# Past keys with decays relative to the block's first query, three score banks, two projection banks

## The reference

```python
z = x @ w_in                                   # q, k, v, forget logits, gates, conv and memory columns
logf = log_sigmoid(f + fox_bf)                 # 12 heads
cum = cumsum(logf)                             # per head
s = q @ k.T * 128 ** -0.5 + cum[query] - cum[key]
p = softmax(where(key <= query, s, -inf))      # 12 heads x 128
o_fox = p @ v
c = causal_conv3(c_gate * h_in)                # 1536 channels, width 3
o_mem = softmax(mq @ mk.T / 16) @ mv           # 4 heads x 256, 256 memory tokens
m = sum_i sigmoid(x @ w_merge_i + b_i) * ((o_i * silu(g_i)) @ w_out_i)
y = layernorm(2 ** 0.25 * x + m @ w_o) * ln_g + ln_b
```

## Time and profile before

| what | value |
|---|---|
| time, median of 3 (lowest to highest) | 3447.69 us (3447.4 to 3559.09) |
| the profiled execution's own time | 3459.89 us |
| its span, slowest of 8 cores | 3458.3 us (cores 3434.4 to 3458.3) |
| mean granted TensorE clock, cores | 0.984 to 0.990 |
| PE busy | 3329.8 us, 96% |
| DVE, ACT, POOL busy | 35%, 26%, 25% |

### The profile page before, as it was taken

How to read it: one execution, slowest core, us unless ns; L and a number is a source line. 1 busy time by engine, 2 the same in 40 slices (tenths; PEclk the granted TensorE clock), 3 DMA queues, 4 the chain that set the end, 5 groups by cost and what they waited for, 6 DMA issues and landing times.

```text
span 3458.3 us, 54793 instructions; the slowest of 8 cores (3434.4 to 3458.3 us)
## 1 busy us (share of the span) xinstructions
PE 3329.8 (96%) x18998; PEld 1643.9 (48%) x18998; DVE 1198.0 (35%) x1989; ACT 915.5 (26%) x1571; POOL 860.8 (25%) x1045
## 2 busy tenths in 40 slices
PE   7899999999998999999999999999999999999997
PEld 4555555555544444444444444455544444444443
DVE  0476666667676222222211111111112232111465
ACT  1355555455554111111111111111113331111111
POOL 2233333333334222222200000222221113322233
PEclk9999999999999999999999999999999999999999
DMA  9634333433331313131224443866662115665643
GB/s 166 122 74 81 73 81 70 81 70 71 73 66 33 49 25 49 25 49 25 46 58 104 109 92 81 167 152 141 154 144 48 25 25 126 137 144 140 206 151 118
DMA packets 151702, 315.80 MB, mean 91 GB/s; under 512 B 32112, under 2 KB 57328, under 8 KB 146940
## 3 DMA queue, kind: packets, MB, share of 16 engines
q0 software_dynamic: 39232, 134.54, 24.5%
q1 hardware_dynamic: 112200, 177.76, 17.0%
HBM read 351.46 MB, written 95.32 MB: 129 GB/s over the span
## 4 chain that ended last, share of the span: by engine, by line
PE 88%; DMA 4%; issue 2%; DVE 2%; ACT 2%; POOL 1%; POOLq 0%; ACTq 0%; DVEq 0%; SPq 0%
PE bank L146 88%; DMA m_scr<-mt 1%; DMA xT<-xTp 1%; DMA fv_p<-v 1%; ACT ge L163 1%; DVE st L181 1%; DVE acc L173 1%; POOL aC L173 0%; ACT pt L163 0%; POOL pt L169 0%; DMA wcb<-wcM 0%; ACT k L168 0%; ACT rl L163 0%; POOL mt L173 0%; POOL pt L705 0%
## 5 line engine op out<-in xcount | busy, mean ns | idle before, releaser
L146 PE MATMUL bank<-xT,wcb 128*128 128x512 bf16 (+1 forms) x3840 | 728.2, 343 | 7.1 <-DMA wcb<-wcM 6.5
L146 PE MATMUL bank<-xT,cwb 128*128 128x512 bf16 (+1 forms) x3840 | 702.5, 343 | 8.9 <-DVE us L173 8.1
L146 PE MATMUL bank<-xT,wkqg 128*128 128x512 bf16 (+1 forms) x2880 | 608.3, 348 | 8.7 <-DMA wkqg<-wkqg 5.0
L146 PEld LDWEIGHTS bank<-xT,wcb 128*128 128x128 bf16 x3840 | 327.1, 98 | 370.3 <-issue 13.5
L146 PEld LDWEIGHTS bank<-xT,cwb 128*128 128x128 bf16 x3840 | 325.1, 98 | 373.4 <-issue 16.4
L173 DVE TENSOR_TENSOR mt<-bank,gt 128x512 f32<-128x512 f32 (+1 forms) x240 | 143.5, 598 | 1032.5 <-PE bank L146 883.5
L163 ACT ACTIVATE pt<-st,ncc 128x512 bf16<-128x512 f32 (+4 forms) x492 | 314.8, 647 | 427.0 <-DVE st L181 352.0
L163 ACT ACTIVATE gt<-bank,bm 128x512 f32<-128x512 f32 (+1 forms) x240 | 147.0, 612 | 969.0 <-PE bank L146 965.0
L146 PEld LDWEIGHTS bank<-xT,wkqg 128*128 128x128 bf16 x2880 | 245.4, 99 | 274.1 <-issue 35.2
L181 DVE SCALAR_TENSOR_TENSOR st<-bank,cq 128x512 f32<-128x512 f32 x480 | 291.3, 608 | 201.0 <-PE bank L146 172.9
L173 DVE TENSOR_TENSOR acc<-acc,pt 128x512 f32<-128x512 f32 (+3 forms) x396 | 260.7, 658 | 0.9 <-POOL pt L705 0.4
(11 more groups left out here) (137 smaller groups left out, 2543.8 us busy)
## 6 DMA issues: line engine op xcount, KB each, us to landing
m_scr<-mt SPq DMA_DIRECT2D x128, 256.0 KB, 2.2
pv<-m_scr SPq DMA_DIRECT2D x128, 256.0 KB, 5.5
cwb<-wc POOLq DMA_DIRECT2D x12, 2048.0 KB, 16.8
wkqg<-wkqg POOLq DMA_DIRECT2D x11, 1536.0 KB, 15.1
mw<-wm POOLq DMA_DIRECT2D x16, 1024.0 KB, 13.9
x<-xp SPq DMA_DIRECT2D x16, 1024.0 KB, 7.2
y_p<-rr SPq DMA_DIRECT2D x16, 1024.0 KB, 4.8
wcb<-wcC POOLq DMA_DIRECT2D x16, 896.0 KB, 10.8
```

The source lines that it names most:

```text
L146: return lambda e: e.matmul(out, lhsT=lhsT, rhs=rhs, start=start, stop=stop)
```

## The change

- **Scores of past keys.** For a tile that lies wholly before its block, the decay is taken relative to the block's first query: a bias column `nb = ncc + cq[first]`, made on POOL a block (a head) ahead by `make_bias`, so ACT takes the exponential straight from the score bank, with no step on DVE. Diagonal tiles keep the old path. The two parts of a block have output banks of their own; before the first diagonal tile `acc` is scaled by `fq = exp(cq - cq[first])` (`make_decay`, ACT), and at the end the past part's output too, and the parts are added (DVE). The sample's cache tile gets eight exponentials of 64 columns, and its two parts are joined in the same way; `csd` goes.
- **Banks and order.** Score banks 2, 3, 7 (three), projection banks 0, 1 (two) in the attention stage; the sample's output takes a projection bank for its time (`held`). `LA` is 4. A head's blocks come as 0, (sample), 1, 3, 2, in head 0 with the sample after 1; `POS` gives the buffers, `past_block` follows. `st` has 2 buffers, `pt` 9.
- **Block ends.** `hi` is copied on DVE; `lo` is due one tile earlier; Ln and Exp of `rl` are recorded a tile apart. A gate's third and fourth step are due one and two tiles after the first two.
- **Caches.** `load_cache` of the next head follows the sample's value tile (now early in a head), for head 0 the start of the stage.
- **Convolution.** The sample's four groups go one after each 512-token block, with buffers of their own.
- **Layer norm.** The last chunk (the sample) is centred, scaled and stored in four quarters over DVE, ACT and POOL.
- **Prologue.** `q_group(0, 3)` comes before the transposes of the forget logits; rows of `wv0` in SBUF are 288 wide, 268 of them used. `masknegb` was not used and goes.

```diff
-    wvf = [bw("wv0", [128, 16 * 268], BF16, r_vw[0]), ...
+    wvf = [bw("wv0", [128, 16 * 288], BF16, r_vw[0]), ...
...
+    held = set()
+    pjb = [0, 1, 7]
     def nextbank():
-        b = (0, 1, 7)[pj[0] % 3]
-        pj[0] += 1
-        return b
+        while True:
+            b = pjb[pj[0] % len(pjb)]
+            pj[0] += 1
+            if b not in held:
+                return b
...
+        if now[0] is None:
+            log1p()
+            gate()
+        else:
+            later.append((now[0] + 1, log1p))
+            later.append((now[0] + 2, gate))
...
-    run_all(k_group(0, 3))
+    run_all(k_group(0, 3) + q_group(0, 3))
...
-    NST, NPT = 3, 7
+    NST, NPT = 2, 9
...
+        dg = lambda tb: [(h, tb, kc) for kc in range(4 * tb, 4 * tb + 4)]
+        of = lambda tb: [(h, tb, kc) for kc in range(4 * tb)]
+        one, late = of(1) + dg(1), [(h, 4, 0), (h, 4, 1)]
+        tiles += dg(0) + (one + late if h == 0 else late + one) + of(3) + dg(3) + of(2) + dg(2)
...
+    pjb[:] = [0, 1]
+    NB0 = (0, 0, 4, 12, 24)
...
+    def make_bias(h, tb):
+        p = h % 2
+        if tb == 0:
+            return
+        c0, n, k0 = NB0[tb], (4 * tb if tb < 4 else 8), (0 if tb < 4 else 16)
+        ref, rr = (cq[:, tb * 512:tb * 512 + 1], r_cq[tb]) if tb < 4 else (cqs[p][:, 0:1], r_cqs[p])
+        S.add(POOL, TS(nb[p][:, c0:c0 + n], ncc[:, k0:k0 + n, h:h + 1].rearrange("p a b -> p (a b)"), ref, ALU.add),
+              reads=[rr, r_ncc], writes=[r_nb[p][tb]])
+        c = 4 * p + tb - 1
+        S.add(POOL, TS(nr[:, c:c + 1], ref, -1.0, ALU.mult), reads=[rr], writes=[r_nr[p][tb]])
...
-        sb_ = 2 + take("s", 2)
+        sb_ = (2, 3, 7)[take("s", 3)]
...
+            else:
+                c = NB0[tb] + kc
+                S.add(ACT, ACTF(pt[p][:], banks[sb_][:], AF.Exp, bias=nb[h % 2][:, c:c + 1], scale=SCALE),
+                      reads=[bankr[sb_], r_nb[h % 2][tb]], writes=[r_pt[p]])
...
+            for c in range(8):
+                S.add(ACT, ACTF(pt[p][:, c * NS:(c + 1) * NS], banks[sb_][:, c * NS:(c + 1) * NS], AF.Exp,
+                                bias=nb[h % 2][:, 24 + c:25 + c], scale=SCALE),
...
+    def next_decays(i, h, tb):
+        if h + 1 < H:
+            load_cq(h + 1, tb)
+            later.append((i + 8, lambda: make_bias(h + 1, tb)))
...
+            if kc == 4 * tb - 2:
+                make_decay(h, tb)
+            if kc == 4 * tb - 1:
+                S.add(DVE, TT(A[:], A[:], fq[:], ALU.mult), reads=[rA, r_fq], writes=[rA])
             if last:
-                S.add(POOL, COPY(pt[hi][:], A[:]), reads=[rA], writes=[r_pt[hi]])
+                S.add(DVE, COPY(pt[hi][:], A[:]), reads=[rA], writes=[r_pt[hi]])
...
+                    S.add(DVE, TT(fq[:], banks[Of][:], fq[:], ALU.mult), reads=[bankr[Of], r_fq], writes=[r_fq])
+                    S.add(DVE, TT(fq[:], banks[Ob][:], fq[:], ALU.add), reads=[bankr[Ob], r_fq], writes=[r_fq])
+                    finish_block(h, tb, rl[:], r_rl, fq[:], [r_fq], 512)
-                later.append((i + 2, s1))
+                later.append((i + 1, s1))
                 later.append((i + 3, s2))
+                later.append((i + 4, s2b))
+                later.append((i + 6, s3))
...
         elif kc == 0:
+            Ob = nextbank()
+            held.add(Ob)
...
+            make_decay(h, 4)
             if h + 1 < H:
                 load_cache(h + 1)
...
-    LA = 3
+    LA = 4
...
-        for tb, (t0, tn) in enumerate(TBLK):
+        late = []
+        for tb in (4, 0, 1, 2, 3):
...
+            gs = [group(cmm(1, tb), tn, ev_c), group(cmm(2, tb), tn, ev_h), group(cmm(0, tb), tn, ev_b), group(cmm(3, tb), tn, ev_g)]
+            if tb == 4:
+                late = gs
+            else:
+                out += gs[0] + gs[1] + gs[2] + gs[3] + late[tb]
...
-        past_block = [f0 + 5, f0 + 3 + 6, f0 + 11 + 6, f0 + 25 + 6]
+        past_block = [f0 + 5, f0 + 3 + 6, f0 + 29 + 6, f0 + 13 + 6]
...
-            for tb in (4, 3):
-                fill += q_group(n, tb, past_block[3]) + g_group(n, tb, past_block[3])
+            fill += q_group(n, 4) + g_group(n, 4)
+            for tb in (3, 2):
+                fill += q_group(n, tb, past_block[tb]) + g_group(n, tb, past_block[tb])
...
+            center(0)
+            S.add(DVE, lambda e: e.reciprocal(out=rstd[s][0:tn, :], in_=rstd[s][0:tn, :]),
+                  reads=[r_rstd[s]], writes=[r_rstd[s]])
+            scale(POOL, 0)
+            center(1)
+            scale(POOL, 1)
+            center(2)
+            scale(DVE, 2)
+            center(3)
+            scale(DVE, 3)
+            break
```

More of the change, by code:

```diff
@@ L397, in build @@
     qown, gown = [None] * 5, [None] * 5
+    POS = (0, 1, 3, 2)
     r_qs = [Res("qs0"), Res("qs1")]
@@ L484, in build @@
     k32i, v32i, gei = [0], [0], [0]
+    now = [None]
+    later = []
     d_fl = S.dmasem("fl")
@@ L828, in colsof @@
     def colsof(i):
-        h, tb, kc, first, last = tiles[i]
+        h, tb, kc = tiles[i]
         if tb == 4:
@@ L839, in main_pieces @@
         if h == 0:
+            load_cache(0)
+            for tb in range(1, 5):
+                make_bias(0, tb)
             for i in range(LA):
@@ L940, in ev_g @@
                     S.add(DVE, COPY(sx[:, 0:tn], banks[bk][:, 0:tn]), reads=[bankr[bk]], writes=[r_sx, bankr[bk]])
-                    S.add(ACT, ACTF(sc[:, 0:tn], sc[:, 0:tn], AF.Ln, bias=1.0), reads=[r_sc[k]], writes=[r_sc[k]])
-                    S.add(ACT, ACTF(sc[:, 0:tn], sc[:, 0:tn], AF.Exp, scale=-1.0), reads=[r_sc[k]], writes=[r_sc[k]])
-                    S.add(POOL, TT(sc[:, 0:tn], sc[:, 0:tn], sx[:, 0:tn], ALU.mult), reads=[r_sc[k], r_sx], writes=[r_sc[k]])
-                S.add(POOL, TT(aC[c][:, t0:t0 + tn], conv["tb"][k][:, 0:tn], sc[:, 0:tn], ALU.mult),
-                      reads=[r_tb[k], r_sc[k]], writes=[r_aC[c][tb]])
@@ L946, in conv_pieces @@
-            out += group(cmm(1, tb), tn, ev_c)
-            out += group(cmm(2, tb), tn, ev_h)
-            out += group(cmm(0, tb), tn, ev_b)
-            out += group(cmm(3, tb), tn, ev_g)
+                    S.add(ACT, ACTF(sc[:, 0:tn], sc[:, 0:tn], AF.Ln, bias=1.0), reads=[rsc], writes=[rsc])
+                    S.add(ACT, ACTF(sc[:, 0:tn], sc[:, 0:tn], AF.Exp, scale=-1.0), reads=[rsc], writes=[rsc])
+                    S.add(POOL, TT(sc[:, 0:tn], sc[:, 0:tn], sx[:, 0:tn], ALU.mult), reads=[rsc, r_sx], writes=[rsc])
@@ L1400, in build, with root @@
               reads=[r_stat[s]], writes=[r_stat[s]])
-        S.add(ACT, ACTF(rstd[s][0:tn, :], mv[s][0:tn, 1:2], AF.Sqrt, bias=epsb[0:tn, 0:1]),
-              reads=[r_stat[s], r_one], writes=[r_stat[s]])
-        S.add(DVE, lambda e, s=s, tn=tn: e.reciprocal(out=rstd[s][0:tn, :], in_=rstd[s][0:tn, :]),
-              reads=[r_stat[s]], writes=[r_stat[s]])
+        def root(s=s, tn=tn):
+            S.add(ACT, ACTF(rstd[s][0:tn, :], mv[s][0:tn, 1:2], AF.Sqrt, bias=epsb[0:tn, 0:1]),
+                  reads=[r_stat[s], r_one], writes=[r_rstd[s]])
+            S.add(DVE, lambda e: e.reciprocal(out=rstd[s][0:tn, :], in_=rstd[s][0:tn, :]),
+                  reads=[r_rstd[s]], writes=[r_rstd[s]])
```

281 lines of the change are left out of this document (167 added, 114 removed).

## The result

The changed kernel is slower: median 3499.56 us of five runs against 3450.42 us of five runs of the kernel before beside it, ratio 1.0122, 95% interval 1.0107 to 1.0136. That is above the forecast's range (3362 to 3436), a loss where a gain was forecast, and less than the 2% at which the forecast called a change slower.

What follows compares the result with a forecast made beforehand. PE, busy 3329.8 of 3458.3 us, was taken as the bound, leaving only its idle and slow-clock time to win. The terms sum to -44.5 us, taking 3459.9 to 3415.4, or 3403 at the median; range 3362 to 3436.

Steps and rivals of the forecast that it cites:

- the DMA term: Head borders in attention: next head's caches loaded there lengthen the load burst by a fifth; +4 us (0 to +12).
- Borders: Attention stage, between heads: more score banks, longer lookahead and reordered steps cut PE's waits; -24 us (-12 to -40).
- The five releasers: PE's attention waits on score add, `rl`, POOL's `pt` copies and masks, DVE's low `pt`; 48.3 us without the stage's end.
- The rival in which the wait moves to ACT: Borders stay as long because of ACT's exponentials; attention gains nothing; 3428 us at the median, chance 0.22.
- End of the stage: End of attention: the last row sum no longer waits behind the sample's convolution steps; -4 us (-4.9 to 0).
- Clock: Attention stage: shorter borders leave PE less often at the lower clock; -12 us (-20 to 0) of 29 lost.
- The rival of a denser PE held at 0.81: A quarter of the attention stage drops to clock 0.81, cancelling the gain; 3448 us at the median, chance 0.03.
- Two projection banks: Attention projections: small groups wait for evictions, three hand-overs a head; +11 us (0 to 63).
- The rival on two banks: Hand-overs cost 1.9 us each, 63 us, plus clock loss; 3499 us profiled, 3487 at the median, chance 0.05.
- Convolution: Convolution stage: sample matmuls' evictions are covered, chunks 57.2 us apart instead of 58.2; -10 us (-6 to -11.8).
- Tail: Kernel end: last chunk's layer norm and store in quarters over several engines; -7.5 us (-8.5 to -5.5).
- Prologue: Kernel start: `q_group(0, 3)` fills PE's wait for forget logits, against slower `wv0` loads; -2 us (-3.5 to 0).

Runs made afterwards that it cites:

- weights earlier: Changed kernel with the wkqg and wv loads put ahead of the head's first tile, caches left in place; ratio 0.9997 to the kernel before.
- weights later: Changed kernel with the wkqg and wv loads behind the head's 28th tile instead of the 2nd; ratio 0.9890 to the kernel before.
- one exponential: Changed kernel with the sample tile's bias added on DVE and one ACT exponential instead of eight; ratio 1.0063 to the kernel before.

## Why the prediction was wrong, point by point

- **The step that failed is the DMA term.** It counted bytes ("the burst at the border grows by a fifth") and gave +4 (0 to +12). Measured is +64.7 us of PE's wait for `v` (66.2 - 1.5). The step priced the cache load, which costs nothing in the old order, and left out what the tiles moved to the border do to two queues. On POOL's they put a mask that waits for eight exponentials on ACT ahead of the weight loads, which then go out 3.4 us ahead of the V groups and not 9.7; the runs that move the loads alone (weights earlier, weights later) show that this place costs 43 to 80 us. On SP's they put two small transfers ahead of the `v` stores, among the loads; the trace shows these, but no run parts them from the first. POOL's queue was named for the bias columns, not for the loads. The stall itself was known, with its releaser; the step took it for a fixed quantity, where it depends on what is in flight within a few us.
- **Borders,** -24. The five releasers fell from 48.3 us without the end of the stage to 7.8 (4.4 + 3.2 + 0.2 of `pt` on DVE); ACT's `pt` took 24.0 of it back: -16.5, inside the range. The rival in which the wait moves to ACT describes this part, and one exponential takes 22 us off that wait. The eight exponentials were priced too low: 3.17 us, not 2.5.
- **End of the stage,** -4: not won, the last row sum stands 4.30 us behind `sx` now.
- **Clock,** -12: none of it. The mean went the other way, from 0.97 to 0.95; after the stall shown it was at the lower level of 1.2 GHz (0.50 at 516 to 520 us). With the weights later it is 0.99, with one exponential besides 1.00. PE's busy time in the stage says what that is worth: 897.5 us before, 899.2 changed, 870.0 in the last. So nearly all of the 29 us could be had; the forecast left out the stretches at 0.81, and in that last run no window of 4 us shows them. The rival of a denser PE held at 0.81 has no support: at its densest the stage was granted 1.00. (Its sum is a little off too: 3459.9 - 44.5 + 47 is 3450 at the median, not 3448.)
- **Two projection banks,** +11. In the kernel before it costs 22 us, twice the term and within its ends; the hand-overs were under-counted, as the gate's eviction was thought covered and `gr` costs 7.4. In the changed kernel they show as 5.8 for `k` and 1.1 for `gr`, but a third bank, taken from the scores, hid 20 of the 66 us of stalls. The term's reading of a bank as a hand-over missed that it is also a reserve against stalls. The rival on two banks had the side right and the mechanism only in part. That its 3499 in the profile meets the measured 3499.8 is luck: it had 63 us of hand-overs, which measured about 7, and no stalls on stores.
- **Convolution,** -10: -11, and 57.4 us a chunk where 57.2 was forecast. Right.
- **Tail,** -7.5: -3.1. Between `rstd` and the last of DVE's steps 6.3 us passed (3486.19 to 3492.47), not 4.3, as two of them took 1.50 and 1.74 instead of 0.69 beside POOL, and the last store still needed some 5.7 to the end.
- **Prologue,** -2: the wait for the forget logits is gone, but PE's wait for `xT` at the start is 24.5 us instead of 20.5; in other runs of the kernel before and its variants it was 21.7 to 24.5, so no gain or loss can be read. The loads of `wv0` did land later with the gaps: after 15.1 to 17.2 us (the median of a run) in the eleven kernels that have them, after 12.8 to 14.5 in the four without.

Of the signs named beforehand, the missing wait for `rl`, the convolution's spacing and the waits behind `k` came, the clock did not, and the end was 14.2 us after the last matmul, not 9 to 10. Of the signs for a wrong forecast, idle time before projections passed 30 us, before the V groups; ACT is the releaser at the border, but with 2 us a head (24.0 over 12), not near 3.

## What to carry to other kernels

When tiles are moved, follow every queue on which something waits for them, and look at what stands behind on those queues, the issue of large loads above all: here a small mask on POOL delayed up to 2.5 MB of weights into the stretch where another transfer was due, and 48 KB of the sample in small packets stood ahead of that transfer on SP's queue. Price a transfer by what is in flight when it starts, not by the bytes added: the same cache load cost nothing at 5.6 us ahead of the V groups in the old order, about 25 us at 3 behind weights still under way, and no wait of DVE at 3.3 with the weights long landed. A load that is needed only a head later belongs in a stretch that stores little; moving it there was worth 2.3% in the changed kernel, and 5 to 15 us in the kernel before by a single run.

## What the runs showed of the hardware

A store of 256 KB that goes out among the weight loads, with small transfers ahead of it on its queue, takes several times as long as without them: `fv_p` lands after 2.0 us at the least, 9.0 in the median and 16.1 at the most over the changed kernel, 3.2 in the median with the weights later. The Trainium skill ("DMA: Bandwidth & Descriptors", Queues, rings and completion order) says that each DMA engine takes turns between the queues that have work, a packet at a time. The trace agrees: from 502 to 512 us the loads' queue moved 293 packets and SP's 290. As the loads' packets have up to 4 KB and the sample's 256 or 128 bytes, equal turns were 1.13 MB against 0.06 MB here.

At the end of the kernel, DVE's steps on 64x512 take 0.68 to 0.74 us alone, but 1.50 and 1.74 while POOL's additions run beside them (3487.94 to 3491.08). POOL's take 1.57 each, where a quarter of the whole row's 4.49 would be 1.12. So cutting one step over the two engines did not give the sum of their speeds. The Trainium skill ("SBUF — State Buffer", SBUF: two separate sides) says that DVE and GpSimd share one pair of ports, and that an instruction of DVE with two inputs in SBUF and one of GpSimd that reads SBUF exclude each other for their whole length. Both steps here are of these kinds, and the rows agree with it; no run here tried the two apart.
